# Feed-forward gate/up projections: 17 of 22 tile pairs computed as seven block products, with two of four weight-block sums made by accumulating DMAs

## The reference

```
hf = rms_norm(x, norm_ffn[l])
gate, up = jnp.split(hf @ w_ffn_in[l], 2, axis=-1)
x = x + (jax.nn.silu(gate) * up) @ w_ffn_out[l]
```

## Time and profile before

| | |
|---|---|
| median of 3 runs | 1576.23 us (1576.15 to 1577.49) |
| profiled execution: span from the first to the last instruction | 1574.7 us |
| PE (TensorE matmuls) busy | 1565.2 us, 99% |
| DVE (VectorE) busy | 913.5 us, 58% |
| ACT (ScalarE) busy | 641.9 us, 41% |
| POOL (GpSimd) busy | 68.1 us, 4% |
| DMA | 155.64 MB, mean 99 GB/s |

### The profile page before, as it was taken

One profiled execution on the slowest core, in us unless ns is written; L12 is line 12 of the kernel. 1 busy time (PEld: TensorE's weight loads), 2 busy tenths in 40 slices (PEclk: granted clock), 3 DMA queues, 4 the chain that ended last, 5 costly groups with the idle time before them and its releaser, 6 DMA issues.

```text
span 1574.7 us, 19003 instructions
## 1 busy us (share of the span) xinstructions
PE 1565.2 (99%) x7372; PEld 1293.9 (82%) x7372; DVE 913.5 (58%) x1353; ACT 641.9 (41%) x1001; POOL 68.1 (4%) x58
## 2 busy tenths in 40 slices
PE   9999999999999999999999999999999999999998
PEld 7877777788888888888888888898888888888887
DVE  6776878666645445357787445455655544434435
ACT  5455766643222222255454334343444332222314
POOL 0000000020000000040000010010001000000002
PEclk9999999999999999999999999999999999999999
DMA  5433232343232323222221242344122332332222
GB/s 191 123 104 100 82 95 74 101 140 94 94 107 91 96 94 107 82 95 96 81 67 60 75 134 87 113 133 135 60 94 94 108 98 95 94 107 94 94 84 77
DMA packets 48522, 155.64 MB, mean 99 GB/s; under 512 B 6064, under 2 KB 7472, under 8 KB 48304
## 3 DMA queue, kind: packets, MB, share of 16 engines
q1 hardware_dynamic: 48128, 153.90, 31.0%
q10 hardware_dynamic: 304, 0.52, 0.1%
HBM read 148.11 MB, written 2.10 MB: 95 GB/s over the span
## 4 chain that ended last, share of the span: by engine, by line
PE 98%; DVE 1%; ACT 0%; DMA 0%; issue 0%; SPq 0%; DVEq 0%; ACTq 0%
PE G L1010 85%; PE SC L1010 4%; PE O L1010 2%; PE TP L1010 2%; PE M L1010 2%; PE TP L1361 1%; PE TP L1305 1%; DMA RAW<-in_va 0%; PE TP L1410 0%; DVE WL L1919 0%; ACT WH L1448 0%; DVE MGl L1919 0%; DVE RAW L2479 0%; DVE T L2193 0%; PE M L1185 0%
## 5 line engine op out<-in xcount | busy, mean ns | idle before, releaser
L1010 PE MATMUL G<-XGh,WH 128*128 128x512 f32 x1248 | 492.6, 395 | 0.0
L1010 PE MATMUL G<-XGh,WL 128*128 128x512 f32 x1248 | 486.3, 390 | 0.0
L1010 PE MATMUL G<-XGl,WH 128*128 128x512 f32 x1248 | 485.9, 389 | 0.0
L1919 DVE TENSOR_TENSOR WL<-RAW,WH 128x1024 fp32r<-128x1024 f32 (+3 forms) x281 | 337.8, 1203 | 190.8 <-ACT WH L1448 190.2
L1448 ACT ACTIVATE WH<-RAW 128x1024 fp32r<-128x1024 f32 (+3 forms) x281 | 283.8, 1011 | 185.0 <-PE G L1010 173.6
L1010 PEld LDWEIGHTS G<-XGh,WH 128*128 128x128 f32 x1248 | 234.3, 188 | 54.5 <-issue 6.2
L1010 PEld LDWEIGHTS G<-XGh,WL 128*128 128x128 f32 x1248 | 234.2, 188 | 49.8
L1010 PEld LDWEIGHTS G<-XGl,WH 128*128 128x128 f32 x1248 | 234.5, 188 | 46.4
L1010 PE MATMUL G<-MGh,WH 128*128 128x512 f32 x400 | 155.9, 390 | 0.0
L1010 PE MATMUL G<-MGl,WH 128*128 128x512 f32 x400 | 155.6, 389 | 0.0
L1010 PE MATMUL G<-MGh,WL 128*128 128x512 f32 x400 | 155.6, 389 | 0.0
(11 more groups left out here) (317 smaller groups left out, 1796.9 us busy)
## 6 DMA issues: line engine op xcount, KB each, us to landing
RAW<-in_up SPq DMA_DIRECT2D x32, 512.0 KB, 3.5
RAW<-in_dn SPq DMA_DIRECT2D x32, 512.0 KB, 3.5
RAW<-in_fg SPq DMA_DIRECT2D x22, 512.0 KB, 3.5
RAW<-in_fu SPq DMA_DIRECT2D x22, 512.0 KB, 3.5
RAW<-in_g SPq DMA_DIRECT2D x16, 512.0 KB, 3.6
RAW<-in_f SPq DMA_DIRECT2D x16, 512.0 KB, 3.5
X<-in_x SPq DMA_DIRECT2D x16, 256.0 KB, 4.1
RAW<-in_q SPq DMA_DIRECT2D x8, 512.0 KB, 3.6
```

Of the source, the lines that this page charges most:

```text
L1010: return e.matmul(dst, st, mv, start=start, stop=stop, skip_group_check=True)
L1919: return e.tensor_tensor(dst, src, hi.bitcast(F32), ALU.subtract)
```

## The change

Pairs 5 to 21 no longer run as 2 x 24 matmuls of 512 columns. The gate/up weights of a pair are seen as four blocks (gate and up, each with the lower and the upper 512 input features), the activations as four blocks too (lower and upper features, tokens 0 to 255 and 256 to 511). The 2 x 2 block product is formed from seven block products (`st` items, j = 0 to 6) instead of eight. Each is 4 x 3 = 12 matmuls of 128 x 256, so a pair has 84 of them. The first operand of a product is a half tile of weights (128 x 512) or a sum of half tiles:

- `t1` = gate lower + up lower, `t3` = up lower + up upper: a plain load from SyncE, and then DMAs issued by GpSimd that add the second half tile to it in SBUF, each in two DMAs of 64 partitions (`fetch_add`)
- `t2` = `t1` + up upper, `t4` = `t2` + gate upper: additions on VectorE (`tile_sum`)

The second operand is a block of the fully normalised activation (`h`, in `Vh`/`Vl`) or one of four sums of such blocks (in `QK`), made once, in four rounds `kt` = 0 to 3 of the steps `h`, `s13`, `s2`, `s4`, `s_hi`, `s_lo`, `a_hi`, `a_lo`. These rounds stand among pairs 0 to 4 (`DIRECT` = 5), which still run directly with 512 columns. The seven products go to five banks of PSUM (`O`, `M`, `TP`, `SC`) in place of `G`, and the four output blocks are formed by subtractions of 128 x 256 on VectorE (`w_less`, `v_less`, `c22`, `c12`, `c21`) and by accumulation in PSUM; ScalarE copies the product j = 2 out (`one_out`) before j = 4 is added to its bank, and takes Silu of the finished gate blocks (`c11`, `silu`). Then comes the product (`z_mul`) and its split.

Weights of the whole feed-forward are handled in half tiles ("items") of 128 x 512 in ten slots (six halves of `WH`/`WL` and four of `WTh`/`WTl`), prepared six items ahead. The hidden values' second buffer is `XGh`/`XGl` in place of `Vh`/`Vl`. A leftover option, splitting weights on GpSimd, is taken out.

```diff
+DIRECT = 5
+SLOTS, AHEAD = 10, 6
+HALF_S = S // 2
...
-    u += [(nm, f, 1024) for f in range(16) for nm in ("fg", "fu")]
-    u += [("f0", n, 1024) for n in range(8)]
-    u += [(nm, f, 1024) for f in range(16, 22) for nm in ("fg", "fu")]
-    u += [("f1", n, 1024) for n in range(8)] + [("f2", n, 768) for n in range(8)]
...
+    t = []
+    for f in range(DIRECT):
+        t += plain("fg", f, 1024) + plain("fu", f, 1024)
+    t += [("st", f, j, S) for f in range(DIRECT, 16) for j in range(7)]
+    for n in range(8):
+        t += plain("f0", n, 1024)
+    t += [("st", f, j, S) for f in range(16, 22) for j in range(7)]
+    for n in range(8):
+        t += plain("f1", n, 1024)
+    for n in range(8):
+        t += plain("f2", n, 768)
...
+        for q, (name, n, part, _) in enumerate(self.items):
+            if name == "st" and part == 0:
+                side = n % 2
+                behind = self.item_of["st", n - 2, 6] + 1 if ("st", n - 2, 6) in self.item_of else 0
+                new = n - 2 < DIRECT or n in (16, 17)
+                out.append(("sums", n, 2, max(behind, held.get(2, 0)) if new else behind))
+                out.append(("pair", n, side, max(behind, held.get(side, 0))))
+                held[side] = q + 7
+                last_pair = q + 7
+            elif name != "st" and part == 0:
+                third = (len(self.units) + n_plain) % NRAW if name in ("fg", "fu") else n % NRAW
+                out.append((name, n, third, max(held.get(third, 0), last_pair if third == 2 else 0)))
+                held[third] = q + 2
+                n_plain += 1
+        return out
...
+    def prepare(self, upto):
+        while self.rounded < min(upto, len(self.items)):
+            name, f, j, _ = self.items[self.rounded]
+            if name == "st" and j in (0, 5):
+                self.put("tile_sum", f, j // 5)
+            self.put("item_hi", self.rounded)
+            self.rounded += 1
+    def settle(self, upto):
+        while self.rest < min(upto, self.rounded):
+            self.put("item_lo", self.rest)
+            self.rest += 1
+            self.fetch()
+    def item(self, name, n, part):
+        q = self.item_of[name, n, part]
+        self.prepare(q + AHEAD + 1)
+        self.settle(q + AHEAD)
...
+        for j in range(7):
+            self.tick()
+            if j == 0:
+                for n, kind in ((3, "one_out"), (3, "w_less"), (3, "v_less"), (4, "c22"), (5, "c11"), (6, "c12"), (7, "c21"),
+                                (8, "silu"), (9, "z_mul"), (10, "z_hi"), (11, "z_lo")):
+                    self.later(n, kind, f)
+            self.put("seventh", f, j, self.item("st", f, j))
...
     def ffn(self):
-        def pair(f):
-            self.gemm("fg", f, ("fg", f))
+        for f in range(DIRECT):
             if f == 0:
...
+                for kt in range(4):
+                    for kind in ("h", "s13", "s2", "s4"):
+                        self.later(3 + 3 * kt, kind, kt)
+                    self.later(4 + 3 * kt, "s_hi", kt)
+                    self.later(4 + 3 * kt, "s_lo", kt)
+                    self.later(5 + 3 * kt, "a_hi", kt)
+                    self.later(5 + 3 * kt, "a_lo", kt)
+            self.pair(f)
+        for f in range(DIRECT, 16):
+            self.seven(f)
+        self.drain()
+        self.residuals("f0", range(8))
         for f in range(16, 22):
-            pair(f)
-        for n in range(8):
-            self.residual("f1", n, n, ("residual", "f1", n))
+            self.seven(f)
+        self.drain()
+        self.residuals("f1", range(8))
         for n in range(HALVED):
-            self.residual("f2", n, n, ("residual", "f2", n))
+            self.residuals("f2", (n,))
...
+                    if name == "sums":
+                        b = b_tiles(n)
+                        if TURN7[n] == 0:
+                            e.wait_ge(prep_dve, PREP_DVE["a_lo", 2])
+                        elif TURN7[n] == 1:
+                            e.wait_ge(prep_dve, PREP_DVE["s_lo", 3])
+                        e.dma_start(b["t1"], a["fg"][n][:, 0:S]).then_inc(d_t1[n % 2], 16)
+                        e.dma_start(b["b22"], a["fu"][n][:, S:2 * S]).then_inc(d_b22[n % 2], 16)
+                        e.dma_start(b["t3"], a["fu"][n][:, 0:S]).then_inc(d_t3[n % 2], 16)
+                    else:
+                        c = 768 if name == "f2" else 1024
+                        e.dma_start(RAW[:, third, 0:c], a["fg" if name == "pair" else name][n]).then_inc(d_raw[third], 16)
...
+                    bank = (OM[n % 2], TP[:, 0, :], SC[:, n % 2, :], TP[:, 1, :], SC[:, n % 2, :], OM[n % 2], TP[:, 1, :])[j]
+                    bank = bank[:, 0:HALF_S]
...
+                    elif j == 4:
+                        e.wait_ge(seven_act, SEVEN_ACT["one_out", pairs[n]])
+                    elif j == 5:
+                        e.wait_ge(seven_dve, SEVEN_DVE["v_less", pairs[n]])
+                    else:
+                        e.wait_ge(seven_dve, SEVEN_DVE["c22", pairs[n]])
...
+                        mm(bank, wh[:, at], hi, start=(kt == 0 and j < 4))
+                        mm(bank, wh[:, at], lo)
+                        if kt == 0:
+                            e.wait_ge(i_lo, q + 1)
+                        t = mm(bank, wl[:, at], hi, stop=(kt == 3))
...
+                elif kind == "one_out":
+                    n = TURN7[arg[0]]
+                    if n > 0:
+                        e.wait_ge(seven_dve, SEVEN_DVE["c22", pairs[n - 1]])
+                    e.wait_ge(i_done, taken("st", arg[0], 2))
+                    hi(ONE_OUT, SC[:, n % 2, 0:HALF_S]).then_inc(seven_act, 1)
...
+                elif kind == "c11":
+                    f = arg[0]
+                    table(ACT.Silu)
+                    e.wait_ge(u_done, FU[f - 2])
+                    e.wait_ge(i_done, taken("st", f, 4))
+                    e.activation(T[:, f % 2, 0:HALF_S], SC[:, TURN7[f] % 2, 0:HALF_S], ACT.Silu).then_inc(seven_act, 1)
...
+                elif kind == "fetch_add":
+                    f = fetches[arg[0]][1]
+                    b, k = b_tiles(f), TURN7[f] // 2
+                    for tile, loaded, added, more in (("t1", d_t1[f % 2], t1_added[f % 2], slice(0, S)),
+                                                      ("t3", d_t3[f % 2], t3_added[f % 2], slice(S, 2 * S))):
+                        e.wait_ge(loaded, X_LOAD + 16 * k + 16)
+                        for r in (slice(0, P // 2), slice(P // 2, P)):
+                            e.dma_start(b[tile][r, :], a["fu"][f][r, more], accum_op=ALU.add).then_inc(added, 16)
...
+                    if TURN7[f] + i > 0:
+                        e.wait_ge(t_sum, 2 * TURN7[f] + i)
+                    if i == 0:
+                        e.wait_ge(t1_added[f % 2], 32 * k)
+                        e.wait_ge(d_b22[f % 2], X_LOAD + 16 * k)
+                        e.tensor_tensor(b["t2"], b["t1"], b["b22"], ALU.add).then_inc(t_sum, 1)
+                    else:
+                        e.wait_ge(d_raw[f % 2], 16 * RAW_LOADS["pair", f])
...
+                elif kind == "h":
+                    kt = arg[0]
+                    if kt == 0:
+                        e.wait_ge(r_done, NRM["norm", "ffn"])
+                    elif kt >= 2:
+                        e.wait_ge(prep_dve, PREP_DVE["a_lo", kt - 2])
+                    for i, k in enumerate((kt, 4 + kt)):
+                        t = e.scalar_tensor_tensor(halves_of(kt)[0][:, i, :], X[:, k, :], gain(G_FFN, k), RB[:, :],
+                                                   ALU.mult, ALU.mult)
...
+                elif kind == "s_lo":
+                    kt = arg[0]
+                    e.wait_ge(prep_act, PREP_ACT["s_hi", kt])
+                    lo(sums_to(1, kt), SUMS, sums_to(0, kt)).then_inc(prep_dve, 1)
+                elif kind == "a_lo":
+                    kt = arg[0]
+                    e.wait_ge(prep_act, PREP_ACT["a_hi", kt])
+                    lo(Vl[:, kt::4, :], halves_of(kt)[0], Vh[:, kt::4, :]).then_inc(prep_dve, 1)
...
+                elif kind == "w_less":
+                    f = arg[0]
+                    if TURN7[f] > 0:
+                        e.wait_ge(seven_dve, SEVEN_DVE["c21", pairs[TURN7[f] - 1]])
+                    e.wait_ge(seven_act, SEVEN_ACT["one_out", f])
+                    e.wait_ge(i_done, taken("st", f, 1))
+                    e.tensor_tensor(W_LESS, TP[:, 0, 0:HALF_S], ONE_OUT, ALU.subtract).then_inc(seven_dve, 1)
...
+                elif kind == "z_mul":
+                    f = arg[0]
+                    s_, u_ = T[:, f % 2, :], T[:, 2 + f % 2, :]
+                    e.wait_ge(seven_act, SEVEN_ACT["c11", f])
+                    e.wait_ge(seven_act, SEVEN_ACT["silu", f])
+                    e.wait_ge(seven_dve, SEVEN_DVE["c12", f])
+                    e.tensor_tensor(u_, u_, s_, ALU.mult).then_inc(u_done, 1)
...
```

372 lines of the change are left out of this document (309 added, 63 removed).

## The result

The changed kernel takes 1666.95 us (1664.33 to 1668.22, 4 runs), the kernel before on the same chip 1576.19 (1575.59 to 1577.49, 4 runs): ratio 1.0573, 95% interval 1.056 to 1.0587. The forecast was 1572.2 us, the range ended at 1592. So it is 94.8 us above the forecast, and the sign is wrong.

A forecast was written before the change was run, and what follows sets the result against it. TensorE was taken as the bound (busy 1565.2 of 1574.7 us). 1574.7 - 14.0 + 8.7 + 1.3 = 1570.7 us of span, 1572.2 us with the 1.5 around it; 8-in-10 range 1563 to 1592.

The forecast's parts named there:

- Removed matmul time: TensorE in the 17 seven-product pairs: 10.06 us per pair in place of 10.88, 14.0 us gone in all.
- VectorE per pair: Added additions and splits in each of 17 pairs: 8.5 to 9.6 us, below TensorE's 10.06, so no stall booked.
- The accumulating DMAs: GpSimd's adding DMAs in each pair: hidden behind 10 to 11 us of lead; 0 us taken, bounds 0 and 19.
- The DMA share: Busy share of DMA in the seven-product pairs: from 0.30 to about 0.6, with no queue of more than a pair.
- The activation sums: Four rounds on VectorE among pairs 0 to 4 delay bank takes: TensorE waits 8.7 us, bounds 0 and 12.
- Before the down projections: ScalarE's `one_out` late at pairs 15 and 21, behind a down unit's first half: 1.3 us together, bounds 0 and 4.
- The clock: Clock gives way only where TensorE rests several us; waits are at most 3.1 us, so nothing added.
- the rival with late DMAs: Adding DMAs late in the pairs: 1572.2 + 0 to 19 us, up to 1591; chance 0.10.
- Held-up VectorE: Rival: GpSimd's DMA work slows VectorE's additions in the pairs, 19 to 44 us, 1591 to 1616; chance 0.12.
- The first rival: Activation sums among pairs 0 to 4 cost nothing: 1576.2 - 14.0 + 0 to 3, given as 1562 to 1567; chance 0.20.

The follow-up runs named there:

- run 2: Changed kernel without the adding DMAs, second half tiles never added (34 weight sums left out): 1572.55 us, ratio 0.9978.
- run 13: Changed kernel, complete, descriptor memory 768 for 256, mask tile 384 columns, VectorE's due weight splits ahead of the next pair's sum: 1573.99 us, ratio 0.9987.
- run 1: Changed kernel with descriptor memory 768 for 256, mask tile 384 columns, part of the mask left out: 1578.3 us, ratio 1.0012.
- run 4: Changed kernel with plain copies in place of adding DMAs, small descriptor memory kept, sums of weights left out: 1573.44 us, ratio 0.9986.
- run 5: Changed kernel, complete, descriptor memory 512 for 256, whole mask read from a 384-column tile: 1580.02 us, ratio 1.0024.
- run 6: As run 5, but each half tile added by one DMA of 128 partitions in place of two of 64: 1584.19 us, ratio 1.0052.
- run 7: As run 2, with activation sums spread out: six direct pairs for five, rounds four ticks apart for three: 1567.07 us, ratio 0.994.
- run 3: Changed kernel with a pair's two half-tile sums made by two GpSimd additions, no adding DMA, nothing left out: 1585.74 us, ratio 1.0059.
- run 15: Changed kernel, small descriptor memory, VectorE making all four sums per pair, weight splits ahead of sums, activation sums spread over six direct pairs: 1573.12 us, ratio 0.9981.
- run 14: As run 13, with the activation sums spread out over six direct pairs: 1577.84 us, ratio 1.0009.
- run 16: As run 14, with seven direct pairs (`DIRECT = 7`) in place of six: 1576.69 us, ratio 1.0003.

## Why the prediction failed

**Removed matmul time, right.** A pair takes 10.08 us where nothing is late (runs 2 and 13), forecast 10.06.

**VectorE per pair, right.** In run 2 TensorE never waits for `c22` or a split; VectorE's spare time ahead of `w_less` is 1.35 us per pair, forecast 0.5 to 1.5.

**The accumulating DMAs: this step failed**, in three places. (1) "I take 0, since nothing in the code makes the second wait for the first": nothing in the code of the engines does, but the memory for descriptors, a number in the kernel's constructor, does. Runs 1, 4, 5 and 6 show it. (2) I wrote of two adding DMAs per pair, while the same step counts 0.5 MB of adding DMAs, which is four of 128 KB, and the page's row has 68 for 17 pairs. One at a time that is 4 x 3.4 to 4 x 4.6 us, more than a pair. (3) I priced lateness against a deadline of 10 to 11 us. It is a loop instead: the loads wait for a split that stands in VectorE's queue behind the sum of the pair before (run 13), which leaves 10.06 less 1.4, some 8.6 us. The third is worth 4.3 us with the large memory and 6.7 with the small one, of 95; the first two are the rest. With four of them, one at a time, my own 4.3 per DMA would have made 4 x 4.3 = 17.2 us a pair (16.4 measured) and 17 x 7.1 = 121 us; the upper end of 19 us was the price of half a pair's DMAs. The DMA share, forecast at about 0.6, is 0.73 in run 1 (1290 to 1350) and 0.59 in run 4: adding costs the DMA engines more than its bytes.

By the formula of the Trainium skill (DMA: Bandwidth & Descriptors, "Anatomy of one DMA") such a DMA takes 2.3 us, an estimate. The trace differs: 3.2 in the median to landing, and up to 6.9. Four in series by the estimate would be 9.2 us, still inside a pair; from start to start they took 16.4 / 4 = 4.1 each. And no time per DMA tells how many may be under way.

**The activation sums: right in place and, by two errors that nearly cancel, in size.** The takes were forecast to end at 1221.3, 1227.8, 1234.3, 1242.7, 1248.5, 1257.1 and 1262.5. After, the first, fourth and last of them (start and length):

```profile
1219.07 0.68 DVE L2785 TENSOR_TENSOR T<-G,RB 128x512 f32<-128x512 f32 x1
...
1240.71 0.68 DVE L2776 TENSOR_TENSOR T<-G,RB 128x512 f32<-128x512 f32 x1
...
1260.64 0.68 DVE L2785 TENSOR_TENSOR T<-G,RB 128x512 f32<-128x512 f32 x1
```

They end at 1219.75, 1241.39 and 1261.32, all within 1.6 us and with the same gaps. But TensorE's waits in this stretch are 60 - 54.60 = 5.4 us in the changed kernel and 60 - 53.34 = 6.7 in run 2, not 8.7; the granted clock there is 0.97, for which I had nothing, and 0.03 x 60 = 1.8 us is an estimate of its price. Together that is 8.5 in run 2. Run 7, with a clock of 1.00, gets 5.5 + 0.8 = 6.3 us back of the 8.7.

**Before the down projections:** forecast 1.3 us, without adding DMAs 0.4.

**The clock:** "the waits above are at most 3.1 us, [...] so I add nothing" failed even for the forecast case: in run 2 the granted clock falls to 0.5 at 1257.3, behind a rest of TensorE of 3.0 us that ended at 1256.0, and in the changed kernel at 1241.6, behind one of 2.7 us. And the rival with late DMAs carried no clock term, where a third of the loss is clock (30.3 of 94.6 us).

**The rivals.** The late DMAs had the right place and the wrong size. Held-up VectorE is refuted for DMAs (0.69 beside them) and true for GpSimd's additions (run 3). The Trainium skill (SBUF — State Buffer, "SBUF: two separate sides") says that a VectorE instruction with two SBUF inputs contends only with a GpSimd instruction that reads SBUF; the traces agree on both. The first rival's sum was off: 1576.2 - 14.0 + 0 to 3 is 1562 to 1565, not 1567.

## What to carry to other kernels

Before costing a DMA that GpSimd issues at its latency, ask how many may be under way at once, and look at the descriptor memory that the kernel sets aside: an engine idle on "issue" ahead of each DMA is its sign. Count a step's DMAs from its bytes, multiply by the time of one if they can only go one by one, and compare with the period; only then look for loops through the release of the load. An engine with 1.35 us to spare per round of 10 can take two additions for 0.17 us a round (10.25 for 10.08, runs 15 and 13); a transfer with enough descriptor memory cost nothing in the rounds, but more at the start, where its result was wanted soonest.

## What the hardware showed that I had not expected

- Adding DMAs of 64 rows under way at once: one with a descriptor memory of 256, three with 512, five with 768 (once each in runs 14 and 16, where a sixth waited); of 128 rows, one with 512. Plain copies of 64 rows: three with 256.
- An issue costs GpSimd 0.82 us for an adding DMA, 0.52 for a plain one of the same size; 0.87 for twice the rows.
- An adding DMA takes twice the share of the DMA engines of a plain one for the same bytes (3.6% and 1.8%).
- A VectorE addition or subtraction of 128 x 512 with both inputs in SBUF lasts 1.46 to 1.78 us beside a GpSimd addition of the same size, and 0.69 beside a DMA issue.
